# Prompt attention in pairs of query tiles, and the chunk mask as contraction rows

## The reference, cut to what matters

```
fox: 4 heads of 64, causal by frame,  logits q k / 8 + cum_q - cum_k
mla: 8 heads, queries and keys of 64 + 32 (rotary), block-causal:
     mask = (pos_k // 64) <= (pos_q // 64)
swa: 4 query heads on 2 key heads, own chunk of 64 and the two before, bias table, sinks
p = softmax(where(mask, logits, -1e30));  out = p v
x = x + concat(fox, mla, swa) @ W_out;  then an MLP
```

## Time and profile before

| | us |
|---|---|
| median of 3 runs | 2944.52 (2942.9 to 2945.08) |
| the profiled execution | 2942.14 |
| its span, first to last instruction | 2940.3 |
| TensorE busy | 2789.0 (95%) |
| VectorE busy | 1777.7 (60%) |
| ScalarE busy | 1077.1 (37%) |
| GpSimd busy | 1024.3 (35%) |
| prompt attention, layer 1 | from 243.9 to 555.9 |
| prompt attention, layer 2 | from 1688.2 to 1998.9 |

### The profile page before, as it was taken

One profiled execution on the slowest core, in us unless ns is written; L12 is line 12 of the kernel. 1 busy time (PEld: TensorE's weight loads), 2 busy tenths in 40 slices (PEclk: granted clock), 3 DMA queues, 4 the chain that ended last, 5 costly groups with the idle time before them and its releaser, 6 DMA issues.

```text
span 2940.3 us, 40047 instructions
## 1 busy us (share of the span) xinstructions
PE 2789.0 (95%) x15094; PEld 2227.9 (76%) x15094; DVE 1777.7 (60%) x2533; ACT 1077.1 (37%) x1894; POOL 1024.3 (35%) x501
## 2 busy tenths in 40 slices
PE   7999999889999999999999999998899999999995
PEld 5985666678788887888789666667778888788884
DVE  3126777633745649888740467775256564688884
ACT  3224554432332333333332354444243233333333
POOL 2110000012644456777511100000145444567765
PEclk9999999999999999999999999999999999999997
DMA  5210000531334346443131100013323433654331
GB/s 202 61 55 14 23 8 16 158 129 72 116 123 155 128 156 255 142 140 128 57 122 55 47 15 15 16 42 131 129 93 128 155 128 125 252 178 139 128 118 71
DMA packets 164389, 310.68 MB, mean 106 GB/s; under 512 B 24704, under 2 KB 89504, under 8 KB 164256
## 3 DMA queue, kind: packets, MB, share of 16 engines
q1 hardware_dynamic: 159936, 301.82, 29.5%
q10 hardware_dynamic: 4320, 7.08, 0.7%
HBM read 206.42 MB, written 102.44 MB: 105 GB/s over the span
## 4 chain that ended last, share of the span: by engine, by line
PE 85%; DVE 7%; issue 3%; ACT 3%; POOL 2%; DMA 0%; ACTq 0%; DVEq 0%; POOLq 0%; SPq 0%
PE ps L2456 7%; PE ps L2460 7%; PE ps L2458 7%; PE ps L2366 7%; PE ps L2367 7%; PE ps L2368 7%; PE ps L2132 6%; PE ps L1990 5%; PE ps L1988 5%; PE ps L1989 5%; PE ps L2185 4%; PE ps L2162 4%; PE ps L2104 2%; PE ps L2247 1%; PE ps L2316 1%
## 5 line engine op out<-in xcount | busy, mean ns | idle before, releaser
L935 POOL TENSOR_TENSOR w_lo<-w_raw,w_hi 128x1024 fp32r<-128x1024 f32 (+2 forms) x32 | 70.1, 2193 | 1039.9 <-ACT w_hi L1091 1039.9
L2456 PE MATMUL ps<-wq_hi,sa_hi 128*128 128x512 f32 x896 | 350.1, 391 | 5.3 <-DVE x L1921 5.3
L2458 PE MATMUL ps<-wq_lo,sa_hi 128*128 128x512 f32 x896 | 349.8, 390 | 0.0
L2460 PE MATMUL ps<-wq_hi,sa_lo 128*128 128x512 f32 x896 | 349.8, 390 | 0.0
L1921 DVE TENSOR_TENSOR x<-ps,x 128x1024 f32<-128x1024 f32 x224 | 264.1, 1212 | 56.5 <-PE ps L2460 51.7
L1859 DVE TENSOR_TENSOR sa_lo<-ra,sa_hi 128x1024 fp32r<-128x1024 f32 x112 | 281.0, 2510 | 23.7 <-ACT sa_hi L1353 23.7
L975 POOL TENSOR_TENSOR wq_lo<-wsum,wq_hi 128x1024 fp32r<-128x1024 f32 x64 | 157.4, 2460 | 290.9 <-ACT wq_hi L1333 290.9
L1988 PE MATMUL ps<-w_hi,hT_hi 128*128 128x512 f32 (+2 forms) x672 | 248.4, 370 | 0.1
L1990 PE MATMUL ps<-w_hi,hT_lo 128*128 128x512 f32 (+2 forms) x672 | 246.2, 366 | 0.0
L1989 PE MATMUL ps<-w_lo,hT_hi 128*128 128x512 f32 (+2 forms) x672 | 245.2, 365 | 0.0
L1851 DVE TENSOR_TENSOR cq<-ps,cq 128x1024 f32<-128x1024 f32 x48 | 58.7, 1222 | 286.3 <-ACT cq L1394 244.2
(11 more groups left out here) (317 smaller groups left out, 6380.8 us busy)
## 6 DMA issues: line engine op xcount, KB each, us to landing
ra<-hidden_scratch SPq DMA_DIRECT2D x112, 512.0 KB, 3.3
hidden_scratch<-cq SPq DMA_DIRECT2D x94, 512.0 KB, 2.7
rq<-in_w_up_dram SPq DMA_DIRECT2D x64, 512.0 KB, 3.8
rq<-in_w_down_dram SPq DMA_DIRECT2D x64, 512.0 KB, 4.3
residual_scratch<-x SPq DMA_DIRECT2D x36, 512.0 KB, 4.7
x<-residual_scratch SPq DMA_DIRECT2D x36, 512.0 KB, 6.6
w_raw<-in_w_in_dram SPq DMA_DIRECT2D x16, 512.0 KB, 5.0
mixer_scratch<-omixT SPq DMA_DIRECT2D x16, 512.0 KB, 2.6
```

The lines of the kernel that those rows point to most:

```text
L2456: pe.matmul(out, ah[:, k, :], bh[:, k * 512:(k + 1) * 512], start=new and k == 0, stop=False, skip_group_check=True)
L2458: pe.matmul(out, ah[:, k, :], bl[:, k * 512:(k + 1) * 512], start=False, stop=False, skip_group_check=True)
L2460: last = pe.matmul(out, al[:, k, :], bh[:, k * 512:(k + 1) * 512], start=False, stop=final and k == 1, skip_group_check=True)
```

## The change

Tiles 2 and 3, 4 and 5, 6 and 7 form pairs for fox and mla. Their units alternate in the list, even tile first. The two units of a pair are one job: they are transposed together, after the second, with blocks (even tile, b), (odd tile, b) side by side in the chunks and the odd tile's last key tile at the end. One value product of 256 columns then serves both tiles, and one of 128 adds the odd tile's last key tile. From tile 4 on a group is two jobs, four units. The windows (swa) of both tiles follow fox, and the rest of mla follows these. The mask product of mla goes; the operands get eight more contraction rows: row b of the keys is 1 in the second half of key tile b, row t of the queries of tile t is -1e30 for the first 64 queries. The key rows are loaded once per layer, the query rows per tile.

```diff
+QK_X = QK_M + 8
 for _t in range(NPT):
-    _rest = [("q1", _t, 0, 0)] + _fox[:2] + [("q2", _t, 0, 0)] + _fox[2:] + _swa
...
+    if joined(_t) != _t:
+        continue
...
+    _fox = [u for both in zip(tile_units("fox", _t), tile_units("fox", _t + 1)) for u in both]
+    _mla = [u for both in zip(tile_units("mla", _t), tile_units("mla", _t + 1)) for u in both]
+    UNITS += [("q1", _t, 0, 0)] + _fox[:2] + [("q2", _t, 0, 0), ("q1", _t + 1, 0, 0)] + _fox[2:4]
+    UNITS += [("q2", _t + 1, 0, 0)] + _fox[4:] + tile_units("swa", _t) + tile_units("swa", _t + 1)
+    UNITS += _mla[:-4] + [("q1", NPT, 0, 0)] * _last + _mla[-4:] + [("q2", NPT, 0, 0)] * _last
...
+def in_pair(u):
+    return UNITS[u][0] != "swa" and UNITS[u][1] >= 2
...
+    _blocks = [(_u, g, b) for g in range(UNITS[_us[0]][3]) for b in key_blocks(_us[0]) for _u in _us]
+    _blocks += [(_us[1], g, UNITS[_us[1]][1]) for g in range(UNITS[_us[0]][3])] if len(_us) == 2 else []
+    JOB_BLOCKS.append(_blocks)
...
+        PLACE[_b] = (_chunks + _i // 4, _i % 4)
...
                 load(wukv[:].rearrange("p h e d -> p (h e d)"), a["w_ukv"][l], tables_in)
+                load(kTm[QK_M:QK_X], c["mask_mla_k"].unsqueeze(1).broadcast_to([NPT, MLA_H, NPT * P]), tables_in)
...
+                query_mask(0)
+                sp.wait_ge(qmask_in.sem, qmask_in.at(l, 16))
+                query_mask(1)
 
                 sp.wait_ge(skew_out.sem, 16)
                 load(bias8[:], ...
...
+                for t in range(NPT - 2):
+                    store_mix(t)
+                    sp.wait_ge(qmask_in.sem, qmask_in.at(l, 16 * (t + 2)))
+                    query_mask(t + 2)
...
         @block.scalar
...
                 for i in range(len(UNITS) + LAG):
-                    if i >= LAG_T and i - LAG_T < len(UNITS) and is_attn(i - LAG_T):
-                        for ch, blocks in chunks_of(i - LAG_T):
+                    if job_ending(i - LAG_T) is not None:
+                        for ch, blocks in chunks_of(job_ending(i - LAG_T)):
...
         @block.vector
...
+                        for k, t in enumerate(tiles):
...
+                            last = nc.vector.tensor_copy(
+                                omixT[t % 2][:, c0:c0 + pairs, :].rearrange("p k n -> p (k n)"),
+                                bank(6 + n % 2)[:, k * pairs * P:(k + 1) * pairs * P])
...
         @block.tensor
...
-                            q, keys, mask = qTm[t % 2][:, h, :], kTm[:, h, :], mmaskB
+                            q, keys, mask = qTm[t % 2][:, h, :], kTm[:, h, :], None
...
+                def probs_transposes(j):
+                    pe.wait_ge(norm_ok.sem, norm_ok.at(l, ATTN[JOBS[j][-1]] + 1))
+                    for ch, blocks in chunks_of(j):
                         if ch >= 2:
                             done = pt_act if ch % 2 else pt_dve
                             pe.wait_ge(done.sem, done.at(l, ch // 2))
...
+                                out = bank(6 + n % 2)[64 * r:64 * r + 64, k // 2 * P:(k // 2 + step) * P]
+                                last = pe.matmul(out, vals[:, b, vh * HD:(vh + 1) * HD],
+                                                 ptb[ch % NPTB][:, i * P:(i + step) * P], start=(b == tiles[0]),
+                                                 stop=(b == tiles[-1]), skip_group_check=True)
+                        if step == 2:
...
+                                last = pe.matmul(bank(6 + n % 2)[64 * r:64 * r + 64, P:2 * P],
+                                                 vals[:, t + 1, h * HD:(h + 1) * HD], ptb[ch % NPTB][:, i * P:(i + 1) * P],
+                                                 start=False, stop=True, skip_group_check=True)
```

More of the change, by code:

```diff
@@ L119, in key_blocks @@
     return key_tiles(UNITS[u][0], UNITS[u][1])
[L124 to L125 removed]
+ATTN = {}
 for _u in range(len(UNITS)):
@@ L141, with tiles_of, job_ending, chunks_of @@
 GROUP_OF = {_u: g for g, us in enumerate(GROUPS) for _u in us}
-TILE_END = [sum(1 for us in GROUPS if UNITS[us[0]][1] <= _t) for _t in range(NPT)]
-NPTB = 8
-def chunks_of(u):
-    blocks = [(g, b) for g in range(UNITS[u][3]) for b in key_blocks(u)]
-    return [(CHUNK0[u] + i, blocks[4 * i:4 * i + 4]) for i in range((len(blocks) + 3) // 4)]
+JOB_OF = {_u: j for j, us in enumerate(JOBS) for _u in us}
+JOB_BLOCKS, JOB_CHUNK0, PLACE = [], [], {}
+_chunks = 0
+for _us in JOBS:
+    _blocks = [(_u, g, b) for g in range(UNITS[_us[0]][3]) for b in key_blocks(_us[0]) for _u in _us]
+    _blocks += [(_us[1], g, UNITS[_us[1]][1]) for g in range(UNITS[_us[0]][3])] if len(_us) == 2 else []
+    JOB_BLOCKS.append(_blocks)
+    JOB_CHUNK0.append(_chunks)
+    for _i, _b in enumerate(_blocks):
+        PLACE[_b] = (_chunks + _i // 4, _i % 4)
+    _chunks += (len(_blocks) + 3) // 4
+NCHUNK = _chunks
+def tiles_of(n):
+    return sorted({UNITS[u][1] for u in GROUPS[n]})
+TILE_END = [1 + max(n for n in range(len(GROUPS)) if t in tiles_of(n)) for t in range(NPT)]
+TILE_FIRST = [min(n for n in range(len(GROUPS)) if t in tiles_of(n)) for t in range(NPT)]
+NPTB = 8
+def job_ending(u):
+    return JOB_OF[u] if 0 <= u < len(UNITS) and u in JOB_OF and JOBS[JOB_OF[u]][-1] == u else None
+def chunks_of(j):
+    blocks = JOB_BLOCKS[j]
+    return [(JOB_CHUNK0[j] + i, blocks[4 * i:4 * i + 4]) for i in range((len(blocks) + 3) // 4)]
 def group_of_chunk(ch):
-    return GROUP_OF[max(u for u in ATTN if CHUNK0[u] <= ch)]
+    return GROUP_OF[JOBS[max(j for j in range(len(JOBS)) if JOB_CHUNK0[j] <= ch)][-1]]
 def group_ending(u):
@@ L338, in hybrid_step @@
         wukv = at("wukv", RING + 20480, [P, MLA_H, 2, HD])
-        qTm = [at(f"qTm{i}", RING + 24576 + i * 4096, [QK_M, MLA_H, P]) for i in range(2)]
+        qTm = [at(f"qTm{i}", RING + 24576 + i * 4096, [QK_X, MLA_H, P]) for i in range(2)]
         omixT = [at(f"omixT{i}", RING + 32768 + i * 4096, [P, KC, P]) for i in range(2)]
@@ L2159, in probs_transposes @@
                             pe.wait_ge(done.sem, done.at(l, ch // 2))
-                        for i, (g, b) in enumerate(blocks):
+                        for i, (u, g, b) in enumerate(blocks):
+                            tiles = key_blocks(u)
                             c0 = (g * len(tiles) + b - tiles[0]) * P
-                            last = pe.transpose(bank(4 + ch % 2)[:, i * P:(i + 1) * P], pbuf[n % 4][:, c0:c0 + P],
+                            last = pe.transpose(bank(4 + ch % 2)[:, i * P:(i + 1) * P], pbuf[ATTN[u] % 4][:, c0:c0 + P],
                                                 identF[:])
@@ L2166, in values @@
                 def values(n):
-                    kind, t, h0, _ = UNITS[GROUPS[n][0]]
+                    us = GROUPS[n]
+                    kind, t, _, _ = UNITS[us[0]]
                     if n >= 2:
                         pe.wait_ge(o_ev.sem, o_ev.at(l, n - 1))
-                    heads = [(u, g) for u in GROUPS[n] for g in range(UNITS[u][3])]
+                    step = len(tiles_of(n))
+                    heads = [(u, g) for u in us[::step] for g in range(UNITS[u][3])]
                     tiles = key_tiles(kind, t)
-                    for ch, _ in chunks_of(GROUPS[n][-1])[-2:]:
+                    for ch, _ in chunks_of(JOB_OF[us[-1]])[-2:]:
                         done = pt_act if ch % 2 else pt_dve
                         pe.wait_ge(done.sem, done.at(l, ch // 2 + 1))
+                    vals = {"fox": Vf, "swa": Vs, "mla": Vm}[kind]
                     for k in range(0, len(heads), 2):
@@ L2181, in values @@
                                 h = UNITS[u][2] + g
-                                ch, i = divmod(g * len(tiles) + b - tiles[0], 4)
-                                vals = {"fox": Vf, "swa": Vs, "mla": Vm}[kind]
+                                ch, i = PLACE[u, g, b]
                                 vh = h // 2 if kind == "swa" else h
[L2185 to L2188, removed]
+                                out = bank(6 + n % 2)[64 * r:64 * r + 64, k // 2 * P:(k // 2 + step) * P]
[3 more added lines that the diff above has]
+                        if step == 2:
+                            for r in range(2):
+                                u, g = heads[k + r]
+                                h, second = UNITS[u][2] + g, us[us.index(u) + 1]
+                                ch, i = PLACE[second, g, t + 1]
+                                last = pe.matmul(bank(6 + n % 2)[64 * r:64 * r + 64, P:2 * P],
+                                                 vals[:, t + 1, h * HD:(h + 1) * HD], ptb[ch % NPTB][:, i * P:(i + 1) * P],
+                                                 start=False, stop=True, skip_group_check=True)
                     last.then_inc(pv_mm.sem, 1)
                 for i in range(len(UNITS) + LAG):
-                    if i >= LAG_T and i - LAG_T < len(UNITS) and is_attn(i - LAG_T):
-                        probs_transposes(i - LAG_T)
+                    if job_ending(i - LAG_T) is not None:
+                        probs_transposes(job_ending(i - LAG_T))
```

(8 more changed lines are left out.)

83 lines of the change are left out of this document (42 added, 41 removed).

## The result

The changed kernel takes 3082.7 us (median of 4 runs, 3078.85 to 3086.36) against 2943.7 before (now also of 4 runs): a ratio of 1.0473, 95% interval 1.0461 to 1.0486. It is 139 us slower; the forecast was 3012 us with a range of 2970 to 3050. The direction was right, half of the size was missed.

What follows compares the result with a forecast made beforehand. TensorE was taken to bound the attention, a second engine close behind. Per layer latent heads +20, forgetting stretch +15, tiles 0 and 1 -1 make 34; two layers 68 on 2942.1 give 3010, 3012 on the median's footing, range 2970 to 3050.

Steps and rivals of the forecast that it cites:

- The clock falls too: Rival, 15%: in the prompt attention a quarter of 270 us runs at half clock, 34 us per layer, half hidden: 3046.
- V: Value products of probabilities: time goes by columns, 0.215 us per 256-column slot; about 3.4 us in tiles 6 and 7.
- Idle: TensorE's idle time in tiles 2 to 7: goes from 10 to some 50 us per layer.
- The stretch of forgetting heads, queries and windows of tiles 6 and 7: Ten bursts per layer with little value work between: waits of 13.3 us in these tiles, +15 us per layer overall.
- S: Score products on TensorE: 1.51 us in tile 6, 1.72 in tile 7.
- The latent turn: Two latent heads of a tile pair: tiles 6 and 7 16.7 us against 14.0, tiles 4 and 5 11.7 against 10.6.
- the replay: Step-by-step timing of two latent heads in tiles 6 and 7 under the new order, ending at 16.67 us.
- wide V is cheap: Rival, 5%: 256-column value products take no longer than 128, saving 20 us per layer, bursts as forecast: 2972.
- Masks: Latent heads' mask products: 64 of 0.06 us go per layer, 3.8 us, 7.6 for both layers.
- Moved loads: Bias and band queued behind the mask loads on SP: at worst 1.6 us late per layer, taken as 0.
- The bursts hide: Rival, 7%: copies come as fast as the transposed chunks, TensorE does not wait, only savings of 14 stay: 2930.
- V and T overlap better: Rival, 8%: the forgetting stretch costs nothing more, -15 us per layer, only the latent turns are lost: 2982.

Runs made afterwards that it cites:

- The filling run: Changed kernel plus two unread products of 512 columns between second and third chunk of bursts with no value products just ahead: 3039.8 us, 1.0324.
- the narrow run: Changed kernel with each value product of 256 columns as two of 128: 3083.5 us, 1.0475.
- two chunks a step: Changed kernel, unit order kept, turning at most two chunks per step, those due first, with a fifth probability buffer: 2984.5 us, 1.0139.
- the masks alone: Kernel before with only the latent heads' chunk mask as eight contraction rows, and the loads this needs: 2931.3 us, 0.9959.
- the run with ScalarE's copies first: Changed kernel with ScalarE's copies of a step ahead of the exponential of the unit before: 3066.1 us, 1.0418.
- the run with halves and window units apart: Changed kernel, third and fourth chunks turned one step later, latent buffer wait moved to ScalarE's exponential, window units among latent groups: 3026.0 us, 1.0287.
- latent pairs alone: Changed kernel with at most two chunks turned per step, five probability buffers, forgetting heads again tile by tile in the old order: 2951.5 us, 1.0027.

## Why the prediction was wrong, point by point

- *The failed step* is the rival "The clock falls too", and the sum that has no term for it. It was given 15% and "a quarter of the 270 us at that level [...] half of it hidden in the waits", 34 us on top of 3012. The trace has 92 us of layer 1 at 0.50, a third of the 270, and none of it is hidden: by the account above the clock costs 38 us beside the idle time, by the same account 35 in layer 2, 73 in all, and 71 are missing. The argument against it was that the clock had held with a wait of 1.64 us. It had not quite: behind that wait and one of 1.1 us the clock was 0.50 from 552.20 to 555.60, where the last V of tile 7 took 3.51 us; that is the missing 0.01 of the 0.99. And the two were the longest of 19 waits, 10 us in all; the change has 51 in layer 1, 51 us in all and up to 2.6 long. The filling run shows that the price is the clock's.
- *Idle* held: "from 10 to some 50 us per layer" came out as 51.1. The stretch of forgetting heads, queries and windows of tiles 6 and 7 was given 13.3; the row 464.80 to 553.00 has 88.20 - 74.80 = 13.4. But it ran at a mean clock of 0.77, so some 40 of its 88 us at 0.50, and the last digit is luck. Piece by piece most waits came as forecast (behind q1 2.0 for 1.95, third chunks behind S 2.3 and 2.6 for 2.45 and 2.65, scores behind the exponential 1.9 for 2.05), but the second q1 brought 1.5 that the sum has not, and a window unit's copy 0.8 instead of 1.95.
- *The latent turn* held, in the two turns that were read (tiles 2 and 3 were not). Tiles 4 and 5: 11.84 at full clock, forecast 11.7. Tiles 6 and 7: 18.40 at 0.91, that is 3.3 us at half clock, 1.7 of them extra, so 16.7 at full clock; forecast 16.67. The chain of waits of that turn:

```profile
571.67 0.60 PE ps L2225 x4
...
572.29 0.59 ACT ptb L1277
...
572.93 1.09 PE ps L2225 x7
574.02 1.52 PE ps L2196 x4
...
577.62 1.23 DVE mx L1717
...
580.27 0.48 ACT ptb L1277
...
580.80 1.72 PE ps L2225 x7
582.51 4.17 PE ps L2196 x8
586.68 3.17 PE ps L2251 x28
589.85 0.22 PE ps L2259 x4
```

  First burst: a short wait for ScalarE's copy, hidden as forecast. Second: third chunk only behind maximum, exponential and copy. S in one at 4.17, where 1.51 and 1.72 make 3.2, is the half clock. A slip of the replay: its maximum of S7 starts at 6.04, while VectorE normalises until 6.12; that is worth 0.1 us a turn.
- *V*: 3.17 + 0.22 = 3.39 in that chain, forecast 3.4, and the narrow run agrees. The rival "wide V is cheap" is out.
- *Masks*: 12.9 instead of 7.6, some 10 of it the masks, in the right direction.
- *Moved loads*: hidden as forecast. The product that waits for the tables starts at 228.90 against 228.59.
- *"The bursts hide" and "V and T overlap better"* are out by the idle time.
- Open: why a lone window unit between pairs costs time with two chunks a step; and whether the latent pairs' last 20 us are their waits alone (some 20 us per layer against 10 with the masks alone) or also the 24 us of half clock; and which waits bring the clock down (the last section).

## What to carry to other kernels

A change that scatters waits of up to 2 or 3 us over a stretch can pay nearly as much again in granted clock, so a forecast needs a term for each. How large the clock's term is can't be read from the sum or the number of the waits: in tiles 2 to 7 of layer 1 the run with ScalarE's copies first has 34 us of idle in 51 waits at a mean clock of 0.87, the run with halves and window units apart 46 us in 39 waits at 0.97, and latent pairs alone 18 of 257 us at 1.00. Work that is joined to feed a wider product comes in larger bursts; if the width buys nothing (here columns set the price), the burst is all that stays. And cut a burst to what its banks hold before reordering the engines that empty them: with a fifth buffer that gave back 98 us here, ScalarE's order alone 17.

## What the runs showed of the hardware

Two things were not expected. Products that nobody reads can pay: 35 us more of them per layer made the kernel 43 us faster. And the clock can fall behind a wait, when the array works again: from 464.80 to 471.70 the array is busy for 5.56 of 6.90 us at 1.00, and then works for 9.55 of 10.20 us at 0.50; likewise 8.25 of 10.00 and then 16.75 of 17.10 in the run with two chunks a step. The low clock is not always free of waits (16.67 of 20.50 us from 519.40). Which waits bring it, no run shows: the kernel before has 0.50 behind its two longest, 1.64 and 1.1 us at the end of tile 7; the run with the masks alone has the same two there and stays at 1.00.
